# Six projection groups of a hybrid attention and expert block: eight half-matrix products per group become seven, with weight sums formed by accumulating transfers

## The chip, the cores and the metric

One core of a Trainium2 chip runs the whole program. The metric is the device time of one execution in microseconds. The kernel before takes 1276.09 us (median of 3 runs, 1275.9 to 1276.17).

## The reference, cut to what matters

x is 256 x 1024 in float32. It is normalised to h, and one matrix product projects h to 11 parts. Two token mixers use them (a gated delta rule in chunks, and a differential softmax attention over 8 heads), their outputs are gated and added, and an output projection and 32 experts of a clamped SwiGLU follow, of which each token uses 4.

```python
h = rms_norm(x, g_mix[l])
proj = h @ w_in[l]
(qa, ka, va, za, beta_in, a_in, qd, kd, vd, gate_a, gate_b) = jnp.split(proj, split_points, axis=-1)
...
oa = gated_delta_rule(qa, ka, va, beta, g)
oa = rms_norm(oa, g_delta_out[l]) * jax.nn.silu(za.reshape(bsz, seq, H_DELTA, DV_DELTA).astype(jnp.float32))
...
od = diff_attention(qd, kd, vd, lam, rel_bias)
...
mix = jax.nn.sigmoid(gate_a + b_gate[l, 0]) * oa + jax.nn.sigmoid(gate_b + b_gate[l, 1]) * od
x = x + mix @ w_o[l]
```

The six groups that the change touches are qd, kd, vd, za, gate_a and gate_b: each is h (256 x 1024) times a 1024 x 1024 block of w_in.

## The kernel before, in words

Five instruction streams run side by side and meet at semaphores. A list `sched`, written out by hand, gives the order of the work; TensorE, VectorE and ScalarE all walk through it in its order and each engine executes its own part of every item. SyncE has its own order, written beside it.

The front has three stages. First 24 "tile" items project the three delta-rule groups (K, Q, V; L1420). Then 48 "pj" items project the other six groups: group g (QD, KD, VD, Z, GA, GB), row block b of 128 tokens and column half n give a product of 8 steps (128 x 128 by 128 x 512, each two instructions on TensorE, L1430). A pj item is 4 of these 8 steps, thus 8 instructions. The results go to PSUM banks 0 and 1 by turns. ScalarE copies them out (L806, L809); for the gates VectorE does (L1169). The waits for a bank are one whole product apart.

The dictionary `after` hangs other work behind each pj item: the chain of the delta rule (`kt`, `vt`, `n2`, `y1`, `y2`, `y3`, `yt`, `s1`, `ks`, `o0`, `qs`, `o1`; each 8 heads of 16 instructions on L1395, followed by a take of PSUM by VectorE or ScalarE), the inverse of the triangular blocks on VectorE (`sb`, eight pieces behind items 3 to 10, L1084 and L1085), the transposes of q and k (`qt`, `ktd`, L1528), their norms (`nq`, `nk`, L1115 and L1121), and per attention head the steps `a1` (logits), `aw`, `a2` and `a3`. When `sb` is done, SyncE stores the inverse to HBM (L496) and loads it back as diagonal blocks (L502); `n2` of item 11 needs them. `odn` and `oan` scale the mixers' outputs (L1146, L1153), `gate_product` (L1002 to L1005) applies the gates, and `mt` turns the mixed result for the output projection w_o (L1574). Then come the residual, the router and the plan of the experts, up to 371 us.

The third stage walks over 32 experts, w_up first (L1719), then w_down (L1766). Their weights arrive in 192 slabs of 2 MB each, through a ring of 11 slots of 16 KB per partition and a twelfth place beside it. Slabs 0 to 10 are loaded in the front, as soon as what lies in their slot is dead (`front_dead`): slots 8, 9 and 6 hold the projection weights (`w_place`, three pieces of 2 MB in turn), slots 8 and 9 hold w_o until its last product (`s_wo` 3 and 4), slot 10 holds h until the router has run. From 375 us on every load waits for the slab before it in the same slot. All of this is issued by SyncE, in order.

GpSimd squares kd and the delta rule's output in the front (L643, L647), scales that output (L652), issues the load of the gate bias (L649), and is idle in most of the rest.

## Time and profile before

| | |
|---|---|
| time, median of 3 runs | 1276.09 us (1275.9 to 1276.17) |
| span of the profiled execution | 1273.7 us |
| TensorE matmul busy | 1229.8 us, 97% of the span |
| VectorE, ScalarE, GpSimd busy | 373.2, 284.8, 45.9 us |
| moved by DMA | 451.94 MB, mean 355 GB/s |
| granted TensorE clock | 0.999 of full speed |

The profiled execution has no time of its own in the list of runs beside its span; the median of the runs lies 2.4 us above that span. Read it so: TensorE is busy nearly all the time, and the DMA queues are at their full rate (428 to 430 GB/s) in all slices after the first 380 us, but not before. Both engines of the chain are near their limit, in different stretches.

### The profile page before, as it was taken

What the parts mean: (1) busy time and instruction counts of PE and PEld (TensorE: products, weight loads), DVE (VectorE), ACT (ScalarE), POOL (GpSimd) and SP (SyncE); (2) the same over time, 40 slices, a digit from 0 to 9 for tenths busy, and PEclk for the clock granted to TensorE, in tenths of its full rate; (3) what the DMA queues carried; (4) which work ended last, traced back from release to release, by engine and by line L of the source; (5) the groups of instructions that cost most, each with busy time, mean ns of one, the idle gap of its engine ahead of it and who ended that gap; (6) DMA issues with size and microseconds to landing.
All of it is one profiled execution on the core that took longest, in us unless ns stands there. A gap on an engine that the chain in (4) does not pass through costs nothing.

```text
span 1273.7 us, 14917 instructions
## 1 busy us (share of the span) xinstructions
PE 1229.8 (97%) x5590; PEld 539.1 (42%) x5590; DVE 373.2 (29%) x1063; ACT 284.8 (22%) x573; POOL 45.9 (4%) x100
## 2 busy tenths in 40 slices
PE   9999999999999999999999999999998989999997
PEld 7777466644443333333333333333333333333332
DVE  5766825666231211111221111221111112211111
ACT  3331212352222121121121112121121211121121
POOL 4400000101000000000000000000000000000000
PEclk9999999999999999999999999999999999999999
DMA  7653431567779999999999999999999999999997
GB/s 255 181 164 129 147 134 67 181 248 264 274 284 417 425 429 429 429 428 430 429 428 427 429 428 428 428 429 429 429 428 428 428 428 429 429 429 429 428 427 314
DMA packets 60764, 451.94 MB, mean 355 GB/s; under 512 B 10600, under 2 KB 13800, under 8 KB 36032
## 3 DMA queue, kind: packets, MB, share of 16 engines
q1 hardware_dynamic: 59176, 447.44, 85.2%
q0 software_dynamic: 1120, 3.56, 1.0%
q10 hardware_dynamic: 440, 0.58, 0.1%
q8 instruction: 16, 0.26, 0.1%
q14 instruction: 12, 0.10, 0.0%
HBM read 449.21 MB, written 1.97 MB: 354 GB/s over the span
## 4 chain that ended last, share of the span: by engine, by line
PE 66%; DMA 19%; DVE 5%; ACT 3%; issue 1%; SPq 1%; DVEq 0%; ACTq 0%
PE pb L1719 20%; DMA space<-in_w_up_dram 19%; PE pb L1766 14%; PE pb L1430 11%; PE pb L1660 4%; PE pb L1420 3%; PE pb L1647 3%; PE pb L1574 2%; PE pb L1395 2%; PE pb L1654 1%; PE pb L1679 1%; DVE buf_a L1334 1%; DVE buf_a L1331 1%; DVE buf_a L1328 1%; ACT buf_a L898 1%
## 5 line engine op out<-in xcount | busy, mean ns | idle before, releaser
L1719 PE MATMUL pb<-space,buf_a 128*64 128x512 f32 x2048 | 460.4, 595 | 15.5 <-DMA space<-in_w_up_dram 15.4
L1719 PEld LDWEIGHTS pb<-space,buf_a 128*64 128x64 f32 x2048 | 146.1, 137 | 284.8 <-issue 257.3
L1766 PE MATMUL pb<-space 128*64 128x512 f32 x1024 | 227.1, 595 | 7.3 <-ACT space L905 7.3
L1328 DVE TENSOR_SCALAR buf_a<-pb 128x256 f32<-128x256 f32 x64 | 27.0, 421 | 686.7 <-PE pb L1719 686.7
L1430 PE MATMUL pb<-space 128*128 128x512 f32 x384 | 171.4, 594 | 0.0
L1766 PEld LDWEIGHTS pb<-space 128*64 128x64 f32 x1024 | 70.7, 137 | 140.9 <-issue 125.3
L1430 PEld LDWEIGHTS pb<-space 128*128 128x128 f32 x384 | 70.3, 190 | 76.1 <-issue 75.1
L881 ACT ACT_TABLE_LOAD x32 | 41.1, 1283 | 222.5 <-PE pb L1647 222.5
L1420 PE MATMUL pb<-space 128*128 128x256 f32 x384 | 88.6, 384 | 0.9 <-ACT space L734 0.5
L1420 PEld LDWEIGHTS pb<-space 128*128 128x128 f32 x384 | 71.3, 190 | 13.1 <-issue 2.4
L898 ACT ACTIVATE buf_a<-buf_a 128x256 f32<-128x256 f32 x64 | 26.7, 417 | 216.7 <-DVE buf_a L1328 216.7
L1660 PE MATMUL pb<-space 64*128 64x512 f32 x264 | 65.6, 615 | 0.8 <-ACT space L907 0.8
L907 ACT COPY space<-pb 128x512 f32<-128x512 f32 x32 | 18.7, 585 | 209.8 <-PE pb L1766 209.8
L1647 PE MATMUL pb<-xt,plan 128*64 128x512 f32 x248 | 58.7, 592 | 0.0
L898 ACT ACT_TABLE_LOAD x32 | 41.1, 1283 | 0.6
L905 ACT COPY space<-pb 128x256 f32<-128x256 f32 x64 | 24.4, 382 | 70.1 <-PE pb L1679 70.1
L982 DVE SCALAR_TENSOR_TENSOR space<-space 128x255 f32<-128x255 f32 (+2 forms) x72 | 36.3, 504 | 2.6
L1647 PEld LDWEIGHTS pb<-xt,plan 128*64 128x64 f32 x248 | 18.9, 137 | 34.3 <-issue 34.3
L1660 PEld LDWEIGHTS pb<-space 64*128 64x128 f32 x264 | 22.8, 186 | 23.1 <-issue 23.1
L1395 PEld LDWEIGHTS pb<-space 128*128 128x128 f32 x240 | 29.0, 192 | 6.2 <-issue 6.2
L1331 DVE TENSOR_TENSOR buf_a<-buf_a 128x256 f32<-128x256 f32 x64 | 27.2, 425 | 9.7 <-ACT buf_a L898 6.7
L1334 DVE SCALAR_TENSOR_TENSOR buf_a<-buf_a 128x256 f32<-128x256 f32 x64 | 27.3, 426 | 7.9
(299 smaller groups left out, 807.3 us busy)
## 6 DMA issues: line engine op xcount, KB each, us to landing
space<-in_w_up_dram SPq DMA_DIRECT2D x127, 2048.0 KB, 25.7
space<-in_w_down_dram SPq DMA_DIRECT2D x61, 2048.0 KB, 24.2
space<-in_w_in_dram SPq DMA_DIRECT2D x17, 2048.0 KB, 8.0
space<-in_w_o_dram SPq DMA_DIRECT2D x2, 2048.0 KB, 11.9
space<-in_w_down_dram SPq DMA_DIRECT2D x4, 1024.0 KB, 27.3
space<-in_w_down_dram SPq DMA_DIRECT2D x4, 512.0 KB, 16.0
space<-in_w_up_dram SPq DMA_DIRECT2D x2, 1024.0 KB, 41.1
xt<-in_x_dram SPq DMA_DIRECT2D x2, 512.0 KB, 5.3
```

The costliest lines, as they stand in the source:

```text
L881: sc.copy(xgt, pb[:, 3, :]).then_inc(s_xgt, 1)
L898: sc.activation(sgm[:, 256 * n_:256 * n_ + 256], glu[:, 256 * n_:256 * n_ + 256], ACT.Sigmoid, scale=ALPHA).then_inc(s_sgm, 1)
L1328: v.tensor_scalar(glu[:, cols], pairs[:, :, 0], LIMIT, None, ALU.min).then_inc(s_glu, 1)
L1331: v.tensor_tensor(sgm[:, cols], sgm[:, cols], glu[:, cols], ALU.mult).then_inc(s_mdve, 1)
L1334: v.scalar_tensor_tensor(out=act[:, cols], in0=lin[:, cols], scalar=1.0, in1=sgm[:, cols], op0=ALU.add, op1=ALU.mult).then_inc(s_actv, 1)
L1395: ins = mm(psA[:, h], lhs(h), rhs(h), start=True, stop=True)
L1420: ins = mm(pb[:, t % 2, 0:T], w[:, c, (t % 4) * P:(t % 4) * P + P], rows[:, c, :], start=(c == 0), stop=(c == KC - 1))
L1430: ins = mm(pb[:, q % 2, :], hT[:, c, b * P:(b + 1) * P], piece_at(n)[:, c, :], start=(c == 0), stop=(c == KC - 1))
L1647: ins = mm(pb[64 * n_:64 * n_ + 64, 3, :], sel[:, b, :], xt[:, b, 512 * n_:512 * n_ + 512], start=(b == 0), stop=(b == NB - 1), skip_group ...
L1660: return mm(pb[:, 4 + 2 * b + n_, :], GT[rows, b * P:(b + 1) * P], ys[rows, :], start=False, stop=True, skip_group_check=True)
L1719: ins = mm(up_out(hf, n_), xg[:, c, :], up_columns(line, hf, n_), start=False, stop=(c == KC - 1), skip_group_check=True)
L1766: ins = mm(pb[64 * hf:64 * hf + 64, 2, :], actT[:, c // 4 * 2 + c % 2, hf_in, :], slot(m)[:, at_:at_ + 512], start=(c == 0), stop=(c == KC ...
```

## The change: what it does

The six groups are computed by a scheme of seven products of half matrices in place of eight (Winograd's form of Strassen's scheme, one level). h is cut into A11, A12, A21, A22 (row block by half of the 1024 inputs), the weight block into B11, B12, B21, B22. Four sums of the A quarters (SA1 to SA4) are formed once, by GpSimd, and lie in the place of x, which is therefore loaded a second time before the residual. The sums of the B quarters are formed per group in the ring: T starts as a plain load of B11 and then takes three accumulating transfers (`grow` 1 to 3), each after the product that reads the state before it; T3 starts as a load and takes one. The accumulating transfers are issued by GpSimd. Per group there are 5 plain and 4 accumulating transfers of 1 MB, in place of 2 plain ones of 2 MB.

48 pj items become 42 "u" items of the same size (4 steps, 8 instructions of L1430's form): P5, P1, P3, P6, P2, P7, P4 in each group. The two PSUM banks alternate with every unit, and some units accumulate on top of what a unit before left there, so each unit waits for a copy or a result of one or two units before. Per group ScalarE copies four partial results (`COPIED`; for the gates VectorE does, with the bias), and VectorE makes the four outputs from them (`group_result`), one each in P6, P2, P7 and P4.

Squares and the scale of the delta rule's output move from GpSimd to ScalarE and VectorE. The attention's steps stand two items earlier, `qt`, `nq`, `nk` and `ktd` one or two; `odn` is cut in two; `mt` stands behind the last two units. Slab 0 and the next are loaded between the quarters; slot 5 waits for the four gate products of Z. Some semaphores are merged.

```diff
+    UNITS = ("P5", "P1", "P3", "P6", "P2", "P7", "P4")
+    U = {name: j for j, name in enumerate(UNITS)}
+    NU = len(UNITS)
+    NG = 6
+    def quarter_place(g, q):
+        if q == "T":
+            return ((8, 0), (6, 1))[g % 2]
+        return {"B11": (8, 1), "B22": (9, 0), "B21": (9, 1), "T3": (6, 0)}[q]
...
-    items_b = []
-    for g in (QD, KD, VD, Z, GA):
-        items_b += [(g, b, n) for n in range(2) for b in range(NB)]
-    items_b += [(GB, b, n) for b in range(NB) for n in range(2)]
-    no_b = {it: i for i, it in enumerate(items_b)}
...
+    put(8, ("qt", 0))
+    put(9, ("qt", 1), ("nq",))
     put(11, ("n2", 0))
     put(12, ("n2", 1))
     put(13, ("y1", 0))
     put(14, ("y2", 0))
...
-    put(15, ("y3", 0))
-    put(16, ("yt", 0), ("nk",))
-    put(17, ("s1",))
-    put(18, ("ks",), ("ktd", 0))
-    put(19, ("y1", 1), ("ktd", 1))
+    put(15, ("y3", 0), ("nk",))
+    put(16, ("yt", 0), ("ktd", 0))
+    put(17, ("s1",), ("ktd", 1))
+    put(18, ("ks",))
+    put(19, ("y1", 1))
...
+    put(28, ("osum",))
+    put(30, ("osc", 0))
+    put(31, ("osc", 1))
     for h in range(H):
-        put(20 + 2 * h, ("a1", h))
-        put(22 + 2 * h, ("aw", h))
-        put(23 + 2 * h, ("a2", h))
-        put(24 + 2 * h, ("a3", h))
+        put(18 + 2 * h, ("a1", h))
+        put(20 + 2 * h, ("aw", h))
+        put(21 + 2 * h, ("a2", h))
+        put(22 + 2 * h, ("a3", h))
+    put(34, ("odn", 0, 6))
+    put(37, ("odn", 6, 8))
+    put(38, ("oan",))
     for i in after:
         after[i].sort(key=lambda it: {"aw": 0, "a2": 0, "a1": 2}.get(it[0], 1))
-    put(46, ("mt", 0), ("mt", 1))
-    put(39, ("odn",))
-    put(41, ("oan",))
+    put(40, ("mt", 0))
+    put(41, ("mt", 1))
...
-        sched.append(("pj", i // 2, i % 2))
+    for i in range(NU * NG):
+        sched.append(("u", i // NU, i % NU))
...
+        A11, A12, A21, A22 = (hT[:, 4 * k:4 * k + 4, P * b:P * b + P] for b in range(NB) for k in range(2))
+        SA1, SA2, SA3, SA4 = (xt[:, b, 512 * i:512 * i + 512].rearrange("p (c t) -> p c t", c=4) for b in range(NB) for i in range(2))
...
+        FACTORS = {"P5": (SA1, "T"), "P1": (A11, "B11"), "P3": (SA4, "B22"), "P6": (SA2, "T"), "P2": (A12, "B21"), "P7": (SA3, "T3"), "P4": (A22, "T")}
+        def bank_of(g, name):
+            return (g + U[name]) % 2
...
+            def load_quarter(g, q):
+                if g == 0:
+                    sp.wait_ge(s_pj, {"B11": 16, "B22": 20, "B21": 21}[q])
+                else:
+                    sp.wait_ge(s_pj, unit(g - 1, {"B11": "P1", "B22": "P3", "B21": "P2"}[q]))
+                sp.dma_start(quarter_at(g, q), w_quarter(g, q)).then_inc(s_q(q), 16)
+            def begin_sum(g):
+                sp.wait_ge(s_pj, (16, 24)[g] if g < 2 else unit(g - 2, "P4"))
+                sp.dma_start(quarter_at(g, "T"), w_quarter(g, "B11")).then_inc(s_tb[g % 2], 16)
+            def begin_third_sum(g):
+                sp.wait_ge(s_pj, unit(g - 1, "P7") if g else 24)
+                sp.dma_start(quarter_at(g, "T3"), w_quarter(g, "B12")).then_inc(s_t3b, 16)
...
+            begin_sum(QD)
+            load_quarter(QD, "B11")
+            load_quarter(QD, "B22")
+            load_quarter(QD, "B21")
+            sp.wait_ge(s_psAf, nA[("kq", 1, 1)] + 1)
+            for b in range(NB):
+                for d in range(4):
+                    q = 32 * b + 8 * d
+                    sp.dma_start(bass.AP(m_dram, q * 1024, [[32, 32], [1024, 8], [1, 32]]), Mt[32 * d:32 * d + 32, b, :, 32 * d:32 * d + 32]).then_inc(s_mst, 16)
+            sp.wait_ge(s_mst, 16 * 8)
+            sp.wait_ge(s_bup, 1)
+            sp.dma_start(ring[0:64, 0, 0:D], m_dram.ap()).then_inc(s_m32, 16)
+            begin_third_sum(QD)
+            begin_sum(KD)
+            for q in ("B11", "B22", "B21"):
+                load_quarter(KD, q)
+            begin_third_sum(KD)
+            begin_sum(VD)
+            for q in ("B11", "B22"):
+                load_quarter(VD, q)
...
+            load_quarter(VD, "B21")
+            begin_third_sum(VD)
+            begin_sum(Z)
+            for g in (Z, GA):
+                for q in ("B11", "B22", "B21"):
+                    load_quarter(g, q)
+                    if g == GA and q == "B22":
+                        front_dead(0)
+                        load(0)
+                begin_third_sum(g)
+                begin_sum(g + 1)
+            load_quarter(GB, "B11")
+            load_quarter(GB, "B22")
+            front_dead(1)
+            load(1)
+            load_quarter(GB, "B21")
+            begin_third_sum(GB)
+            front_dead(2)
+            load(2)
+            sp.wait_ge(s_pj, unit(GB, "P1"))
+            load_w_o(0, 0)
+            load_w_o(0, 1)
+            front_dead(3)
+            load(3)
+            sp.wait_ge(s_pj, unit(GB, "P3"))
+            load_w_o(1, 0)
+            sp.wait_ge(s_pj, unit(GB, "P2"))
+            load_w_o(1, 1)
+            load(4)
+            sp.wait_ge(s_pj, unit(GB, "P7"))
+            for b in range(NB):
+                sp.dma_start(xt[:, b, :], x[0, b * P:(b + 1) * P, :]).then_inc(s_x[b], 16)
...
+            link(pool.tensor_tensor(SA1, A21, A22, ALU.subtract))
+            link(pool.tensor_tensor(SA2, SA1, A11, ALU.subtract))
+            pool.tensor_tensor(SA3, A11, A21, ALU.subtract).then_inc(s_hT, 1)
+            pool.tensor_tensor(SA4, A12, SA2, ALU.add).then_inc(s_hT, 1)
...
+            def grow(g, n):
+                if n == 1:
+                    pool.wait_ge(s_tb[g % 2], 16 * (g // 2 + 1))
+                else:
+                    pool.wait_ge(s_pj, unit(g, ("P5", "P6")[n - 2]))
+                    pool.wait_ge(s_t[g % 2], grown(g, n - 1))
+                pool.dma_start(quarter_at(g, "T"), w_quarter(g, ("B12", "B22", "B21")[n - 1]), accum_op=ALU.add).then_inc(s_t[g % 2], 16)
+            def grow_third(g):
+                pool.wait_ge(s_t3b, 16 * (g + 1))
+                pool.dma_start(quarter_at(g, "T3"), w_quarter(g, "B22"), accum_op=ALU.add).then_inc(s_t3, 16)
+            grow(QD, 1)
+            grow(QD, 2)
+            grow_third(QD)
+            grow(KD, 1)
...
+            grow(QD, 3)
+            for g in range(KD, NG):
+                grow(g, 2)
+                grow_third(g)
+                if g == Z:
+                    pool.wait_ge(s_psA, nA[("y3", 1)] + 1)
+                    pool.dma_start(gbias, b_gate.to_broadcast([P, 2, D])).then_inc(s_ml, 16)
+                if g < GB:
+                    grow(g + 1, 1)
+                grow(g, 3)
...
+            COPIED = {"P5": 2, "P1": 1, "P3": 0, "P7": 3}
+            USED = {"P2": 0, "P7": 1, "P4": 2}
+            LAST_USED = {"P6": 0, "P2": 1, "P7": 2, "P4": 3}
...
+                    if name in COPIED and g < GA:
+                        k = COPIED[name]
+                        act_e.wait_ge(s_pj, unit(g, name))
+                        if name == "P5" and g == VD:
+                            act_e.wait_ge(s_psA, nA[("vt", 1)] + 1)
+                        elif name == "P5" and g == Z:
+                            act_e.wait_ge(s_red, 2)
+                        sc.copy(group_out(g, k), pb[:, bank_of(g, name), :]).then_inc(s_pjf, 1)
+                    if g == GB and name in LAST_USED:
+                        use(g, LAST_USED[name])
+                    elif g < GB and name in USED:
+                        use(g, USED[name])
+                    if name == "P5" and g:
+                        use(g - 1, 3)
...
+            def group_result(g, name):
+                k = RESULT[name]
+                dst, src = group_out(g, k), pb[:, bank_of(g, name), :]
+                dve.wait_ge(s_pj, unit(g, name))
+                if name == "P6":
+                    dve.wait_ge(s_pjf, copied(g, 3))
+                    ins = v.tensor_tensor(dst, dst, src, ALU.subtract)
+                elif name == "P2":
+                    dve.wait_ge(s_pjf, copied(g, 2))
+                    ins = v.tensor_tensor(dst, src, dst, ALU.add)
+                elif name == "P7":
+                    if g < GA:
+                        dve.wait_ge(s_pjf, copied(g, 4))
+                        src = group_out(g, 3)
+                    ins = v.tensor_tensor(dst, dst, src, ALU.subtract)
+                else:
+                    dve.wait_ge(s_pjf, copied(g, 4))
+                    ins = v.tensor_tensor(dst, src, dst, ALU.add)
+                ins.then_inc(s_cf, 1)
...
+                    g, name = it[1], UNITS[it[2]]
+                    if g > Z and name == "P5":
+                        gate_product(g - 1, 2)
+                    if name in RESULT:
+                        group_result(g, name)
+                    if g >= GA and name in COPIED:
+                        if g == GA and name == "P5":
+                            dve.wait_ge(s_ml, 64)
+                        take_with_bias(g, name, COPIED[name])
+                    if g > Z and name == "P1":
+                        gate_product(g - 1, 3)
+                    elif g >= Z and name == "P7":
+                        gate_product(g, 0)
+                    elif g >= Z and name == "P4":
+                        gate_product(g, 1)
+                        if g == GB:
+                            gate_product(g, 2)
+                            gate_product(g, 3)
...
+                    rows, q = FACTORS[name]
+                    bank = bank_of(g, name)
+                    if name == "P5":
+                        if g == 0:
+                            pe.wait_ge(s_pjf, 23)
+                            pe.wait_ge(s_hT, 4)
+                        else:
+                            pe.wait_ge(s_pjf, copied(g - 1, 4))
+                        pe.wait_ge(s_t[g % 2], grown(g, 1))
+                    elif name == "P1":
+                        if g == 0:
+                            pe.wait_ge(s_pjf, 24)
+                        else:
+                            pe.wait_ge(s_cf, 4 * g)
+                        pe.wait_ge(s_q(q), loaded(g, q))
+                    elif name == "P3":
+                        pe.wait_ge(s_pjf, copied(g, 1))
+                        pe.wait_ge(s_q(q), loaded(g, q))
+                    elif name == "P6":
+                        pe.wait_ge(s_pjf, copied(g, 2))
+                        pe.wait_ge(s_t[g % 2], grown(g, 2))
+                    elif name == "P2":
+                        pe.wait_ge(s_pjf, copied(g, 3))
+                        pe.wait_ge(s_q(q), loaded(g, q))
+                    elif name == "P7":
+                        pe.wait_ge(s_cf, 4 * g + 1)
+                        pe.wait_ge(s_t3, 16 * (g + 1))
+                    else:
+                        pe.wait_ge(s_cf, 4 * g + 2)
+                        pe.wait_ge(s_t[g % 2], grown(g, 3))
+                    cols = quarter(g, q).rearrange("p (k n) -> p k n", k=4)
+                    opens = name in ("P5", "P1", "P2", "P4")
+                    for c in range(4):
+                        ins = mm(pb[:, bank, :], rows[:, c, :], cols[:, c, :], start=(opens and c == 0), stop=(c == 3), skip_group_check=True)
+                    ins.then_inc(s_pj, 1)
```

## Rows read from the trace of the kernel before

**Rows 1.** The page: the span, and GB/s in 40 slices of 31.8 us.
```profile
span 1273.7 us, 14917 instructions
...
GB/s 255 181 164 129 147 134 67 181 248 264 274 284 417 425 429 429 429 428 430 429 428 427 429 428 428 428 429 429 429 428 428 428 428 429 429 429 429 428 427 314
```

**Rows 2.** The chain that ended last: start us, us, what; an early pair and late ones.
```profile
426.55 6.87 PE pb L1719 x32
...
481.36 6.87 PE pb L1719 x32
...
921.85 39.52 DMA space<-in_w_up_dram
...
1212.10 38.15 DMA space<-in_w_up_dram
```

**Rows 3.** Windows: stretch, length, busy of PE, PEld, DVE, ACT, POOL, PEclk, DMA share, GB/s.
```profile
260.00:280.00 20.00, 19.29 (x70) 9.79 (x69) 11.83 (x38) 12.79 (x45) 0.00 (x0) 1.00 0.70 276
...
340.00:350.00 10.00, 9.76 (x29) 4.65 (x28) 2.03 (x8) 3.88 (x8) 1.85 (x4) 1.00 0.99 420
350.00:360.00 10.00, 10.00 (x42) 5.85 (x41) 3.15 (x11) 1.79 (x4) 0.00 (x0) 1.00 0.70 250
360.00:370.00 10.00, 9.21 (x54) 5.48 (x52) 6.53 (x29) 3.83 (x10) 0.00 (x0) 1.00 0.70 264
...
380.00:390.00 10.00, 9.62 (x46) 3.50 (x44) 3.10 (x9) 3.98 (x5) 0.00 (x0) 1.00 1.01 433
```

**Rows 4.** Timeline of PE in the front: start us, us, engine line op xcount.
```profile
126.59 24.20 PE L1430 MATMUL pb<-space 128*128 128x512 f32 x56
...
159.25 1.95 PE L1395 MATMUL pb<-space 128*128 128x128 f32 x16
161.03 3.60 PE L1430 MATMUL pb<-space 128*128 128x512 f32 x8
...
329.90 7.03 PE L1574 MATMUL pb<-space 128*128 128x512 f32 x16
...
371.56 7.04 PE L1719 MATMUL pb<-space,buf_a 128*64 128x512 f32 x32
```

**Rows 5.** Timeline of DVE, the inverse (first and last of 31 pairs) and the norm behind it.
```profile
129.07 0.18 DVE L1084 TENSOR_TENSOR space<-space 64x31 f32<-64x31 f32 x1
...
151.71 0.18 DVE L1085 TENSOR_TENSOR space<-space 64x31 f32<-64x31 f32 x1
151.82 2.27 DVE L1115 TENSOR_REDUCE sm<-space 128x32 f32<-128x2048 f32 x1
...
158.60 0.19 DVE L929 TENSOR_TENSOR sm<-sm 128x32 f32<-128x32 f32 x1 [3.90 <-ACT sm L686]
```

**Rows 6.** Timeline of SP's queue: the inverse is stored and loaded back.
```profile
151.93 0.49 SPq L496 DMA_DIRECT2D t_blocks<-space  x1
154.82 3.78 SPq L502 DMA_DIRECT2D space<-t_blocks  x8
```

**Rows 7.** Timeline of DVE, later steps.
```profile
193.49 2.36 DVE L1127 TENSOR_TENSOR space<-space,sm 128x1024 f32<-128x1024 f32 x2
...
277.58 0.69 DVE L1169 TENSOR_TENSOR space<-pb,space 128x512 f32<-128x512 f32 x1
...
306.00 4.29 DVE L1146 SCALAR_TENSOR_TENSOR buf_a<-buf_a,sm,space 128x128 f32<-128x128 f32 x16
...
322.97 0.68 DVE L1004 SCALAR_TENSOR_TENSOR buf_a<-space,buf_a 128x512 f32<-128x512 f32 x1
323.69 0.69 DVE L1005 TENSOR_TENSOR buf_a<-buf_a,space 128x512 f32<-128x512 f32 x1
```

**Rows 8.** DMA of the page and its view: issues, KB each, us from issue to landing.
```profile
q0 software_dynamic: 1120, 3.56, 1.0%
...
space<-in_w_in_dram SPq DMA_DIRECT2D x17, 2048.0 KB, 8.0
...
space<-in_b_gate_dram POOLq DMA_DIRECT2D x1, 1024.0 KB, 6.9
```

313 lines of the change are left out of this document (152 added, 161 removed).

## The prediction

> **What bounds the kernel now.** I read the page first. From the thirteenth slice on the DMA queues move 417 to 430 GB/s in every slice but the last [rows 1]; that is their limit. The chain of waits says the same: from 922 us on its longest pieces are waits for w_up slabs, such as 39.5 and 38.2 us [rows 2]. Until then TensorE runs one expert in 27.4 us (426.55 to 481.36 for a pair [rows 2]), while 12.58 MB of slabs per expert take 29.3 us at 429 GB/s, so the ring, filled in the front, slowly drains. The end is therefore set by when the queues become full for good, plus what is left to move. The windows show that moment: 420 GB/s at 340 to 350 us, then 250 and 264 while slots 8, 9 and 10 are still in use, and 433 from 380 [rows 3]. Those slots, and the refills behind them, are released by TensorE's progress (the last products of w_o, the router, the first expert). So TensorE's front, from 113.7 us (first pj item) to 371.56 us (first expert, [rows 4]), sets the start of the full stream, and a microsecond won or lost there moves the end by one, as long as the queues have nothing left over from the front. In this front TensorE waits for nearly nothing: seven items in a row in 24.2 us, and w_o starts at 329.90, right behind the last item [rows 4].
>
> **Fewer products.** An item of eight instructions takes 3.44 us: 24.04 us for seven [rows 4]. 48 items become 42: 6 x 3.44 = 20.6 us off the path. All work behind the items stays, partly two items earlier, so it takes the same TensorE time. This is the whole gain; everything else can only cost.
>
> **The inverse comes late.** VectorE's 31 pairs of L1084 and L1085 run from 129.07 to 151.89, 22.8 us without a pause [rows 5]. Then SyncE stores (151.93), loads back from 154.82 (four loads of half a row block issued by 156.7), and `n2` starts at 159.25 [rows 4, 6]: some 7 us behind the end of the pairs, with practically no slack. In the new order `n2` still stands behind item 11, and the items before it are equally many and long, with the two `qt` before it as before; TensorE would be there at 159.25 again. But VectorE now has to make results between the pieces of the inverse. The first piece stands behind the result of P6 (item 3), which ends at 126.59 + 3.44 = 130.0, and a result costs 0.69 us like L1169 [rows 7]; so it starts at 130.8. Between the pieces stand three more results of QD (2.1 us, and 1.4 us of waiting for P2's end and for ScalarE's copy of P7), then, ahead of the last piece, `nq` and the result of KD's P6. `nq` took 2.27 us for the reduction and until 159.46 in all, of which 3.90 us waited for ScalarE [rows 5]; ScalarE should now be less late, so I take 4.1 us, and 0.7 for the result. 130.8 + 22.8 + 3.5 + 4.1 + 0.7 = 161.9 against 151.9. With the same way through HBM (6.6 us) `n2` can start at 168.5, 9.2 us late. No other work is queued on TensorE ahead of it. Bounds: 6 us (if `nq` costs only its 2.3 us and the copies are early) to 13 us (`nq` as long as before).
>
> **`nk` before `yt`.** `nk` moves in front of `yt`'s take; `ktd` needs its first half. From the end of `y3` it takes 1.22 (the take) + 2.8 (reduction and two small steps) + 0.6 (ScalarE's root) + 0.9 (four small steps) + 1.2 us (half of the 2.36 us of L1127 [rows 7]) = 6.7 us; TensorE has 3.44 + 1.78 us of work (item, then 159.25 to 161.03 for `yt` [rows 4]). Cost 1.5, bounds 0 to 3.
>
> **The end of the projections.** Before, the gates' last products were covered by a pj item. Now VectorE has, behind item 34, a result (0.7), a gate product (0.7), `aw` (four passes, some 1.8) and twelve of the sixteen operations of `odn` (4.29 x 12/16 = 3.2 us [rows 7]) with its root (1.4), some 7.8 us, and only then the two copies with bias that item 37 waits for: 9.2 us against 7.9 us of TensorE work, cost 1.3. Behind item 40 stand a result, a copy with bias and a gate product of two operations, 0.69 + 0.69 + 1.4 = 2.8 us, before `mt` 0 can run; behind item 41 a result, a gate product, then `mt` 1 and ScalarE's copy, 0.7 + 1.4 + 0.5 + 0.6 = 3.2 us, before w_o can start [rows 7]. Nothing is queued on TensorE to cover these. Together 7.3, bounds 4 to 9. The bank handovers elsewhere have one unit (3.44 us) of cover for a 0.6 or 0.7 us copy; between the heads of the attention VectorE is busy for 11.83 of 20 us, ScalarE for 12.79 [rows 3], and VectorE gets some 1 us per two units more. I take 0; up to 4 if its long items fall badly.
>
> **The transfers.** The before has no accumulating transfer. The nearest row is the gate bias, 1 MB from GpSimd's queue, 6.9 us from issue to landing; 2 MB of w_in land in 8.0 [rows 8]. Lower bound for one: 6.9 us, like a plain one. If the destination has to be read too, it costs the time of 1 MB more at 429 GB/s, 2.4 us: 9.3; upper bound two plain ones in turn, 13.8. I take 9.3, as an addition needs both operands. The windows that the schedule leaves: `grow` 2 two units with what lies behind them (9.4 us in QD), `grow` 3 two units (6.9 us in QD and GB, more between). In QD `grow` 3, issued at 130.2, stands in GpSimd's queue behind T3 and KD's first sum, 4.9 us of data each, issued at about 125 and 127. It lands near 142, 5 us late for item 6, and item 6's result moves the inverse by 3.8. As a plain transfer it would be 0.4 late. In GA and GB the windows of 8 to 10 us meet slabs 0 to 4 and w_o on the other queue (2 MB, 4.9 us each): I take 3 us together, bounds 0 to 12. Sum 6.8, bounds 0.5 to 18. The bytes: 5 more MB-blocks in six groups and x are 32.5 MB or 76 us of full queue, 135 us with second reads. The slices from 64 to 318 us leave room for 156 us [rows 1], so the stream is not delayed at the lower price and hardly at the higher.
>
> The Trainium skill, "Collectives: The Full Stack", the bandwidth ceiling (fold count), says that a reducing transfer is slow because it makes two reads for one write, not because of the addition, with a measured ratio of 1.93. By that rule a chain of such transfers would run at about half the rate, which is the 9.3 us, not the 6.9 us; no row here can show it. The sum with 6.9 us would be 1276.
>
> **The clock.** All windows of the front show a granted clock of 1.00 [rows 3], but none has a wait of 9 us. After this one the next unit and step (3.44 + 1.78) might run at the lower level, 1.2 GHz: 0 to 5.2 us, I take 2. The Trainium skill, "TensorE: Matmul & The Clock Gate", Part 1, states that the clock falls to half when TensorE idles and comes back after work; the rows only show it never idle for long.
>
> **The sum.** -20.6 + 9.2 + 1.5 + 7.3 + 0 + 6.8 + 2 = +6.2 us. The second load of x (1 MB, issued 3.4 us before the last unit ends, needed after the first w_o product, 7 us long, and the 3.2 us before it) and GpSimd's four sums (about 1 us each, at some 60 us, long before item 0) cost nothing; if slabs ahead of x delayed it by more than 4 us, the residual would wait. ScalarE's squares replace GpSimd's, off the path. The profiled span would go from 1273.7 to 1279.9 us; the median lay 2.4 us above the span, 1276.09 + 6.2 = 1282.3.
>
> **Rivals.**
> 1. The handovers on VectorE fit better than I lay them out (the inverse 6 late, the end 4, the rest 0) and accumulating costs as a plain transfer: -20.6 + 6 + 0 + 4 + 0.5 = -10, 1266; with half of these, 1270. For it: ScalarE and VectorE are idle most of the time, and before 240 us the queues are half empty. Against it: the 22.8 us of the inverse are unbroken, and its order behind item 3 is fixed. Chance 0.32, by all cases that end below 1273.5.
> 2. The costs cancel the gain, 1276: the sum with accumulation as cheap as plain, and a steady clock. Chance 0.15.
> 3. The queues decide: an accumulating transfer takes 13.8 us and over, so that in every group `grow` 2 and 3 miss windows of 7 to 9 us by 3 us or more once the other queue is busy. 18 us of transfers in place of 6.8 gives 1294; it decides from a landing time of about 10 us on. Chance 0.15.
> 4. My forecast, 1282.3 (own range 1279 to 1289): 0.38.
> A last one, that the change doesn't do what it says, has no chance worth a number: the items are counted in the schedule.
>
> **How the numbers follow.** Likeliest is case 4. Range: down to 1267 (most of rival 1), up to 1298 (rival 3 with some of the bounds above). A measurement of this kernel tells 0.2%, 2.6 us, from no change: faster 0.32, same 0.15, slower 0.53.
>
> **What would show it.** Right: 336 instructions of the projection in the place of 384; TensorE idle for 6 to 13 us ahead of `n2` with the inverse's end near 162 and the load-back as its releaser; gaps of about 3 us before each `mt` or w_o; the first expert 4 to 9 us later than 371.56. Landing times from GpSimd's queue of 9 us or more support the transfers' term, 7 us refute it. Wrong: an `n2` that starts at 160, or a first expert before 368 us; or a first expert early but an end that isn't, which would mean that the queues carried a backlog over the front.

## The result and the profile after

The changed kernel takes 1348.46 us (median of 4 runs, 1347.71 to 1351.16), the kernel before 1276.13 us on the same chip: ratio 1.0567, 95% interval 1.0552 to 1.0582, 72.3 us slower. The forecast was 1282.3 us with a range up to 1298. The sign was right, the size was wrong by 66 us. In the profiled execution the span grew from 1273.7 to 1346.0 us, also by 72.3.

The page of the kernel after: the span, the clock and the DMA line in 40 slices of 33.7 us, the two large queues, the chain of waits, and the issues (KB each, us from issue to landing).

```profile
span 1346.0 us, 14958 instructions
...
PEclk9999788999789999999999999999999999999999
DMA  8554997898897999999999999999999999999997
GB/s 264 187 137 118 264 211 171 228 279 229 270 340 286 381 428 428 428 428 428 428 428 428 427 428 428 428 428 429 428 428 428 428 428 428 429 428 428 428 428 324
...
q1 hardware_dynamic: 62856, 454.78, 82.0%
q0 software_dynamic: 13792, 28.73, 11.4%
...
PE pb L1955 19%; DMA space<-in_w_up_dram 18%; PE pb L2002 14%; DMA space<-in_w_in_dram 9%; PE pb L1667 6%; PE pb L1896 4%; PE pb L1630 3%; PE pb L1883 3%; PE pb L1810 2%; PE pb L1605 1%; PE pb L1890 1%; PE pb L1915 1%; DVE buf_a L1541 1%; DVE buf_a L1544 1%; DVE buf_a L1538 1%
...
space<-in_w_in_dram SPq DMA_DIRECT2D x31, 1024.0 KB, 12.5
space<-in_w_in_dram POOLq DMA_DIRECT2D x24, 1024.0 KB, 16.4
```

From the fifteenth slice on, the queues are as full as before from the thirteenth [rows 1]. In slices 5 to 12 they are 70 to over 90% busy, yet move only 171 to 340 GB/s: busy, but at a low rate. The chain now holds 9% of waits for w_in, which before it did not name. The 24 accumulating transfers (growths, below) land 16.4 us after their issue (the median); 9.3 us was my price. The page also counts the 336 projection instructions that the change promised, 144 and 192 on L1667, in the place of 384.

The timeline of TensorE from the first item of the new stage to the first expert (start us, us, engine, line, operation, tiles; in brackets the idle time before it and what ended it). It answers [rows 4].

```profile
120.01 3.60 PE L1667 MATMUL pb<-space,xt 128*128 128x512 f32 x8
...
135.74 3.67 PE L1667 MATMUL pb<-space,xt 128*128 128x512 f32 x8 [2.64 <-DMA space<-in_w_in_dram]
...
150.29 6.29 PE L1667 MATMUL pb<-space,xt 128*128 128x512 f32 x8 [7.45 <-DMA space<-in_w_in_dram]
...
165.03 5.75 PE L1667 MATMUL pb<-space 128*128 128x512 f32 x8 [8.45 <-DMA space<-in_w_in_dram]
...
206.03 3.75 PE L1605 MATMUL pb<-space 128*128 128x128 f32 x16 [15.00 <-issue]
...
305.40 5.54 PE L1667 MATMUL pb<-space 128*128 128x512 f32 x8 [6.89 <-DMA space<-in_w_in_dram]
...
352.67 5.79 PE L1667 MATMUL pb<-space 128*128 128x512 f32 x8 [13.70 <-DMA space<-in_w_in_dram]
...
393.55 5.83 PE L1667 MATMUL pb<-space 128*128 128x512 f32 x8 [6.38 <-DMA space<-in_w_in_dram]
...
444.65 7.04 PE L1955 MATMUL pb<-space,buf_a 128*64 128x512 f32 x32
```

The first item starts at 120.0 instead of 113.7, the first expert at 444.65 instead of 371.56 [rows 4]: 73.1 us, and the end moved by 72.3. The whole loss lies in the front. Within the stage TensorE waits some 72 us: 48.5 us for quarters of w_in (the P4 unit of four groups, P7 of the first one, and some small ones) and 15.0 us ahead of `n2` (the row at 206.03). Behind each of the five waits of 6.4 to 13.7 us for w_in eight instructions take 5.5 to 6.3 us instead of 3.6, and behind `n2` sixteen small ones take 3.75 instead of 1.95: that is the lower of the two clock levels (1.2 instead of 2.4 GHz), some 13 us behind six waits. It does not grow with the wait: 2.7 us behind 7.45, 2.2 behind 13.70, and almost nothing (0.07) behind 2.64.

The windows of the same stretches (columns as in [rows 3]) show the granted clock at 0.77 and 0.83 where it had been 1.00:

```profile
150.00:200.00 50.00, 31.19 (x72) 13.90 (x72) 22.39 (x57) 8.20 (x12) 5.17 (x4) 0.77 0.90 213
...
350.00:400.00 50.00, 35.29 (x83) 15.51 (x83) 21.64 (x52) 10.81 (x22) 3.87 (x3) 0.83 0.95 295
```

The DMA view of the whole front (105 to 420 us: bytes and share of the 16 engines' time):

```profile
q1 hardware_dynamic: 22388, 51.67, 45.0%
q0 software_dynamic: 12288, 25.17, 43.3%
...
t_blocks<-space SPq DMA_DIRECT2D x1, 256.0 KB, 9.9
```

GpSimd's queue moved half the bytes of the other and took as much of the engines: 0.433 x 315 = 136 us for 25.17 MB (24 transfers of 1 MB, of which 23 add and one is the gate bias). The 256 KB store of the inverse, which landed within 2.9 us before (SyncE issued the loads back right behind it [rows 6]), took 9.9.

### The profile page after: what moved, and what is told of

Same layout as the page of the kernel before. It is cut to its first block, busy times and chain, and to the rows that moved or that the text cites. A ratio compares the mean times of both kernels' runs of the same rounds, so it can differ in the third digit from the quotient of the medians.

```text
span 1346.0 us, 14958 instructions
## 1 busy us (share of the span) xinstructions
PE 1228.1 (91%) x5542; PEld 537.8 (40%) x5542; DVE 391.3 (29%) x1081; ACT 296.9 (22%) x598; POOL 70.3 (5%) x121
## 3 DMA queue, kind: packets, MB, share of 16 engines
HBM read 481.71 MB, written 1.97 MB: 359 GB/s over the span
## 4 chain that ended last, share of the span: by engine, by line
PE 57%; DMA 28%; DVE 4%; issue 3%; ACT 2%; SPq 1%; POOL 0%; DVEq 0%; ACTq 0%; POOLq 0%
PE pb L1955 19%; DMA space<-in_w_up_dram 18%; PE pb L2002 14%; DMA space<-in_w_in_dram 9%; PE pb L1667 6%; PE pb L1896 4%; PE pb L1630 3%; PE pb L1883 3%; PE pb L1810 2%; PE pb L1605 1%; PE pb L1890 1%; PE pb L1915 1%; DVE buf_a L1541 1%; DVE buf_a L1544 1%; DVE buf_a L1538 1%
## 5 line engine op out<-in xcount | busy, mean ns | idle before, releaser
L1955 PE MATMUL pb<-space,buf_a 128*64 128x512 f32 x2048 | 460.4, 595 | 14.8 <-DMA space<-in_w_up_dram 14.7
L1667 PE MATMUL pb<-space 128*128 128x512 f32 x144 | 73.6, 658 | 35.8 <-DMA space<-in_w_in_dram 35.8
L1667 PE MATMUL pb<-space,xt 128*128 128x512 f32 x192 | 90.2, 614 | 13.5 <-DMA space<-in_w_in_dram 12.8
L1630 PE MATMUL pb<-space 128*128 128x256 f32 x384 | 91.3, 392 | 4.4 <-ACT space L907 4.0
L1630 PEld LDWEIGHTS pb<-space 128*128 128x128 f32 x384 | 73.3, 195 | 17.4 <-ACT space L907 4.3
L1667 PEld LDWEIGHTS pb<-space 128*128 128x128 f32 x144 | 29.4, 213 | 70.4 <-issue 70.2
L1667 PEld LDWEIGHTS pb<-space,xt 128*128 128x128 f32 x192 | 35.9, 197 | 53.9 <-issue 52.3
L1605 PE MATMUL pb<-space 128*128 128x128 f32 x240 | 31.0, 285 | 15.0 <-issue 15.0
L778 POOL DMA_DIRECT2D space<-in_w_in_dram x18 | 26.7, 1485 | 264.2 <-PE pb L1667 240.9
L1152 DVE SCALAR_TENSOR_TENSOR space<-space 128x255 f32<-128x255 f32 (+2 forms) x72 | 39.3, 546 | 2.6
L1605 PEld LDWEIGHTS pb<-space 128*128 128x128 f32 x240 | 30.5, 201 | 21.1 <-issue 21.1
## 6 DMA issues: line engine op xcount, KB each, us to landing
space<-in_w_in_dram POOLq DMA_DIRECT2D x24, 1024.0 KB, 16.4
```

Source lines behind the costliest of these rows:

```text
L1152: ins = v.scalar_tensor_tensor(out=a[:, d:], in0=src[:, 0:T - d], scalar=conv_c[:, 3 - d, tap:tap + 1], in1=a[:, d:], op0=ALU.mult, op1=AL ...
L1605: ins = mm(psA[:, h], lhs(h), rhs(h), start=True, stop=True)
L1630: ins = mm(pb[:, t % 2, 0:T], w[:, c, (t % 4) * P:(t % 4) * P + P], rows[:, c, :], start=(c == 0), stop=(c == KC - 1))
L1667: ins = mm(pb[:, bank, :], rows[:, c, :], cols[:, c, :], start=(opens and c == 0), stop=(c == 3), skip_group_check=True)
L1955: ins = mm(up_out(hf, n_), xg[:, c, :], up_columns(line, hf, n_), start=False, stop=(c == KC - 1), skip_group_check=True)
```

## The experiments

Each row gives the difference of the time from the kernel before on the same chip, the difference of the profiled spans, and the start of the first expert against 371.56. Span and first expert agree within 1.0 us, time and first expert within 1.9: the end follows the front.

| kernel | time | minus before | span minus 1273.7 | first expert minus 371.56 |
|---|---|---|---|---|
| after | 1348.46 | +72.3 | +72.3 | +73.1 |
| f2: inverse one item earlier | 1351.96 | +76.2 | +77.6 | +76.6 |
| f1: four sums later | 1343.06 | +67.3 | +68.7 | +68.4 |
| f3: third growth first | 1337.80 | +62.1 | +63.2 | +63.2 |
| g4: f1, f2 and f3 together | 1329.07 | +52.9 | +53.4 | +53.6 |
| f4: sums on GpSimd | 1321.13 | +45.4 | +46.3 | +45.8 |
| g3: 2 of 4 sums on VectorE, groups 2 to 6 | 1309.60 | +33.4 | +33.4 | +33.2 |
| e2: transfers without addition | 1302.2 (one run) | +25.8 | +26.8 | +26.6 |
| g5: g3 in all groups | 1291.93 | +15.5 | +16.1 | +16.0 |
| g1: no accumulating transfers | 1288.27 | +12.1 | +13.4 | +13.1 |
| g2: g1, and the orders of f1 and f2 | 1271.87 | -4.3 | -1.9 | -2.4 |

### The price of the transfer by itself (e1)

The kernel only moves 1 MB quarters of w_in: plain from SyncE, plain and accumulating from GpSimd, one by one, three in a row, and beside six loads of SyncE's queue.

> A small kernel that computes nothing of the block: it only moves quarters of w_in (1 MB, rows of 2 KB), one after the other. Theory: an accumulating transfer takes more than twice a plain one's data time even alone; in the changed kernel the GpSimd queue was busy for 43.3% of 315 us with 24 of them, 5.7 us of all 16 engines for each, against 2.4 us for 1 MB at 429 GB/s. So 6 to 7 us plain, 10 us or more accumulating, and three issued together take 6 us more for each. Rival (they are only late because of what is queued beside them): 7 us alone, 2.5 us more for each further one.

GpSimd's timeline, where each issue but those of L61 waits for the landing of the one before (L55 plain, L58 accumulating, L61 three accumulating at once, L63 accumulating beside six loads, L66 plain beside six loads, L70 accumulating with 8 KB rows):

```profile
48.10 0.77 POOL L55 DMA_DIRECT2D space<-in_w_in_dram  x1 [5.08 <-DMA space<-in_w_in_dram]
54.02 0.75 POOL L55 DMA_DIRECT2D space<-in_w_in_dram  x1 [5.15 <-DMA space<-in_w_in_dram]
59.69 1.31 POOL L58 DMA_DIRECT2D space<-in_w_in_dram  x1 [4.92 <-DMA space<-in_w_in_dram]
68.62 1.28 POOL L58 DMA_DIRECT2D space<-in_w_in_dram  x1 [7.62 <-DMA space<-in_w_in_dram]
77.24 1.27 POOL L58 DMA_DIRECT2D space<-in_w_in_dram  x1 [7.34 <-DMA space<-in_w_in_dram]
86.17 3.87 POOL L61 DMA_DIRECT2D space<-in_w_in_dram  x3 [7.67 <-DMA space<-in_w_in_dram]
105.22 1.29 POOL L63 DMA_DIRECT2D space<-in_w_in_dram  x1 [15.19 <-DMA space<-in_w_in_dram]
```

Alone, an accumulating transfer lands in 8.6 us, a plain one of the same queue in 5.6, one of SyncE's in 5.1. Three issued 0.75 us apart land 8.5, 12.8 and 17.2 us after their issue, so one landing follows the other by some 5.1 us. Beside six loads, one takes 14.6 (a plain one 9.7). So neither theory had it: alone it is cheaper than the theory's 10 us and dearer than the rival's 7, and each further one lies between their 6 and 2.5 us. The price alone was even under my 9.3; what I had not priced was company. In the changed kernel, company is the rule.

### Where the addition's share lies (e2, g1)

In e2 the 24 transfers overwrite their place instead of adding to it, so the sums of quarters are not formed; bytes read, issues and waits stay.

```diff
-  pool.dma_start(quarter_at(g, "T"), w_quarter(g, ("B12", "B22", "B21")[n - 1]), accum_op=ALU.add).then_inc(s_t[g % 2], 16)
+  pool.dma_start(quarter_at(g, "T"), w_quarter(g, ("B12", "B22", "B21")[n - 1])).then_inc(s_t[g % 2], 16)
```

> The changed kernel with the addition left out of the 24 accumulating transfers: same bytes, same queue, same waits; the last quarter then overwrites the sum, so six projections are wrong. Theory (the second read and the addition are the price): landing times fall from 16.4 to about 8 us, the waits of TensorE for w_in from 48.5 to under 10 us, and the time to 1285 to 1295 us. Rival (the bytes and the software queue are the price, not the addition): stays at 1335 to 1350 us.

It took 1302.2 us (one run), 7 us beyond the theory's range and far from the rival's: 46 us of the 72 go with the addition alone. The transfers landed after 7.8 us and the waits for w_in fell to 8.8 us, both as the theory had them. The engines' share, in the DMA view of its front (105 to 390 us), shows how:

```profile
q1 hardware_dynamic: 22597, 54.17, 52.0%
q0 software_dynamic: 6464, 25.30, 24.3%
```

The same 25 MB take 0.243 x 285 = 69 us of the 16 engines instead of 136, so each MB costs 1.97 times the engines' time when it is added. It is not the crowd that makes it so: in e1, where nothing else runs, three plain transfers take 53.5% of the engines from 42.0 to 59.6 us (9.4 us) and three accumulating ones 71.8% from 59.7 to 86.1 us (19.0 us), twice as much. The Trainium skill, "Collectives: The Full Stack", the bandwidth ceiling (fold count), has a measured 1.93 between the copying and the reducing step of a ring of cores and explains it by two reads for one write; the traces here agree with the ratio for a transfer from HBM to SBUF, and no run here looks at the reads.

In e3 the 24 transfers are left out (the semaphores are raised without them), so the sums are only their first quarters.

```diff
-  pool.dma_start(quarter_at(g, "T"), w_quarter(g, ("B12", "B22", "B21")[n - 1]), accum_op=ALU.add).then_inc(s_t[g % 2], 16)
+  pool.sem_inc(s_t[g % 2], 16)
```

> The changed kernel without its 24 accumulating transfers, their counts raised at once by GpSimd: T stays B11, T3 stays B12, so six projections are wrong. Theory: what is left is the gain of 20.6 us, the early loss of 6.3 us (GpSimd's four sums block VectorE) and VectorE's order (inverse 9.2, ktd 1.5, end 7.3, clock 2): 1282 us, between 1278 and 1286. Rival (VectorE's order costs little, everything was the transfers): 1262 us.

The other values sent more than 64 tokens to one expert, so the kernel went over the experts twice (2227 us), and only its front can be read: first expert at 380.49, 8.9 us late, which fits the theory's 1278 to 1286. g1 is the same kernel with the number of rounds held at one:

> The kernel without the 24 additions (only the first quarter of each sum is loaded, so the outputs of the projections are not the reference's) with the number of rounds over the experts held at one, as in the kernel before, so that its total can be compared. Its first expert started 8.9 us later than before in the trace. Theory (the end follows the front one to one): 1282 to 1288 us. Rival (24 MB of reads less leave the stream a lead that the front doesn't show): under 1280 us.

1288.27 us, ratio 1.0091 (1.0075 to 1.0108): 0.3 us above what the theory gave. Its first expert started at 384.64, 4 us later than in e3 with the same instructions and, within 0.1 us, the same waits. Three rows of g1 show where it went:

```profile
288.17 5.06 PE L1667 MATMUL pb<-space,xt 128*128 128x512 f32 x8
...
332.83 4.83 PE L1667 MATMUL pb<-space 128*128 128x512 f32 x8
...
341.20 8.80 PE L1810 MATMUL pb<-space 128*128 128x512 f32 x16 [0.77 <-ACT space L868]
```

In e3 the same three take 3.70, 3.60 and 7.10 us. With the short rows beside them, g1 lost 1.7 us at each of the three places, 5.1 in all, less the 0.8 us by which it was ahead at 286 us: the granted clock of 280 to 300, 320 to 340 and 340 to 360 us is 0.91 in g1 and 1.00 in e3. So behind the same waits of 2.4 us, of 2.7, and of 2.1 and 0.8 close together, the clock fell in one execution and not in the other. A front with waits in it is thus known only to some 4 us from one profile. In sum: of 72 us, 46 are the addition, 14 (1302.2 to 1288.3) the 24 MB, their issues and their waits as plain transfers, and 12 are there without any of them. Of the 14, e2's timeline shows 8.8 us as three waits for w_in (3.09, 4.54 and 1.14), and most of the rest as more time at the lower clock.

### The queue of three (f3, g4)

After P5 of a group GpSimd issued its second growth, its third sum, and the first growth of the next group; the third growth of this group, needed two items after P6, stood behind them. In f3 the next group's growth comes last.

```diff
                 grow(g, 2)
                 grow_third(g)
-                if g < GB:
-                    grow(g + 1, 1)
                 grow(g, 3)
+                if g < GB:
+                    grow(g + 1, 1)
```

(and for the first group likewise)

> The changed kernel with one edit: the first growth of the next group's sum is queued behind the third growth of the present one instead of ahead of it, so that two accumulating transfers instead of three stand together. Theory (a queue of accumulating transfers, each about 4.4 us more when issued together, and more beside loads): the waits ahead of P4 (8.5, 6.9, 13.7 and 6.4 us in the trace) shrink by 4 to 8 us each, the sum of waits by 15 to 30 us, and the time to 1318 to 1335 us. Rival (it is the traffic of all queues together, not the order): the waits only move from P4 to the next P5, and the time stays within 8 us of 1348.

1337.80 us, ratio 1.0482 (1.0465 to 1.05): 10.7 us less, under what the theory gave (13 to 30) and over the rival's 8. The timeline shows why both are half right:

```profile
157.70 2.81 PE L1667 MATMUL pb<-space 128*128 128x512 f32 x6 [2.36 <-DMA space<-in_w_in_dram]
...
164.52 5.07 PE L1667 MATMUL pb<-space,xt 128*128 128x512 f32 x8 [3.15 <-DMA space<-in_w_in_dram]
...
337.03 3.75 PE L1667 MATMUL pb<-space 128*128 128x512 f32 x4 [8.26 <-DMA space<-in_w_in_dram]
345.11 3.67 PE L1667 MATMUL pb<-space,xt 128*128 128x512 f32 x8 [1.55 <-DMA space<-in_w_in_dram]
```

(The first and the third row are cut at the edge of their window.) The P4 waits fell from 8.45 to 2.36 and from 13.70 to 8.26, and new waits of 3.15 and 1.55 us came at the next P5: part of each wait only moved. All waits for w_in fell from 48.5 to 37.6 us. The order was one cause; the addition itself (46 us in e2) is the larger one.

### GpSimd's four sums (f1)

The four sums of turned quarters, which I had put down as free, move from tile 6 to one behind each of tiles 12 to 15.

```diff
-            link(pool.tensor_tensor(SA1, A21, A22, ALU.subtract))
+            pool.wait_ge(s_pj, 12)
+            link(pool.tensor_tensor(SA1, A21, A22, ALU.subtract))
```

> The changed kernel with one edit: GpSimd's four sums of turned quarters (each 1.27 to 1.44 us, at 55.85 to 61.28 us in its trace) move from the sixth tile to tiles 12 to 15, one behind each tile. Theory (the lock): they cost 6.3 us because they stood where VectorE's chain sets the pace (three of its additions took 4.25 us instead of 1.58); one per tile is absorbed by the pauses of 1 to 2 us that VectorE has per tile, so the first item of the new stage starts 6 us earlier, at 114 us, and the time falls by 5 to 7 us to 1342 to 1344 us. Rival A (the waits on transfers give the time back, since the transfers don't start earlier): the stage starts earlier but the time falls by less than 2 us. Rival B: the lock costs as much at any place: no change.

In the kernel after, VectorE's timeline has this row beside them; the same operations take 1.52 to 1.58 us elsewhere:

```profile
57.31 4.25 DVE L1152 SCALAR_TENSOR_TENSOR space<-space 128x255 f32<-128x255 f32 x3
```

TensorE's timeline shows what came of it:

```profile
67.95 6.52 PE L1630 MATMUL pb<-space 128*128 128x256 f32 x16 [3.97 <-ACT space L907]
```

ScalarE waited for VectorE, and TensorE for ScalarE: 3.97 us, 0.48 before, and the sixteen instructions behind it took 6.52 us at the lower clock, 3.72 before. So 3.5 of the 6.3 us are VectorE's delay, and 2.8 are the clock.

With the move the first item started at 113.59 instead of 120.01, and the time fell by 5.4 us to 1343.06 (ratio 1.0531, 1.0513 to 1.0549), as the theory had it. Where VectorE has pauses, the same four operations cost nothing (113.59 against 113.67 us before).

### The inverse one item earlier (e4, f2)

```diff
-        put(3 + i, ("sb", 4 * i, min(4 * i + 4, 31)))
+        put(2 + i, ("sb", 4 * i, min(4 * i + 4, 31)))
-    put(9, ("qt", 1), ("nq",))
+    put(9, ("qt", 1))
+    put(10, ("nq",))
```

First on top of e3, without accumulating transfers (two rounds again, so only the front counts), then alone in the changed kernel:

> As e3_no_growth, with the eight pieces of the inverse one item earlier (behind items 2 to 9) and nq behind item 10. Theory: n2 waits 3 us in place of 10, the time falls by 6 to 10 us against e3_no_growth. Rival (the inverse is not what n2 waits for, or TensorE's wait there is absorbed elsewhere): no change, within 1 us.

> The changed kernel, accumulating transfers and all, with one edit: the pieces of the triangular inverse stand one item earlier in VectorE's order and the reduction of the first group behind item 10. In the kernel without the 24 additions this moved the first expert 9.3 us forward. Theory: the wait of 15.0 us at n2 falls by 7 to 9 us and the time with it, to 1339 to 1342 us. Rival: the inverse's end is not what is late beside the slow store (9.9 us), or the transfers' waits right behind grow by what n2 gives: under 3 us.

In e4 the wait at `n2` fell from 8.35 to 1.22 us and the first expert came at 371.19, 9.3 us earlier. In f2 it gave nothing: 1351.96 us, 3.5 us more than the kernel after (the runs of the two overlap), with 15.98 us of waiting at `n2`. My theory fell, and SyncE's timeline of f2, with the DMA view of 180 to 204 us, and then the same two rows of the kernel after say why:

```profile
182.78 0.64 SPq L595 DMA_DIRECT2D t_blocks<-space  x1
201.72 3.81 SPq L601 DMA_DIRECT2D space<-t_blocks  x8
```

```profile
q0 software_dynamic: 1792, 3.57, 80.6%
q1 hardware_dynamic: 1136, 2.36, 29.4%
...
t_blocks<-space SPq DMA_DIRECT2D x1, 256.0 KB, 18.9
```

```profile
190.69 0.49 SPq L594 DMA_DIRECT2D t_blocks<-space  x1
200.63 3.89 SPq L600 DMA_DIRECT2D space<-t_blocks  x8
```

The inverse was stored 7.9 us earlier, but it landed no earlier: at 201.7 us, 200.6 in the kernel after. In both, GpSimd's growths hold 80% of the engines around the store. The last of the three issued together from 174.6 us on (174.9 in f2), and the quarter of w_in that stands ahead of the store in SyncE's queue, land only at about 199.5 us (200.5 in f2), and the store some 1 us behind them. It waited for the end of this burst, and an earlier issue only lengthened the wait, from 9.9 to 18.9 us. How much of it is the shared engines and how much the quarter ahead in the same queue, no run separates. In g4, with f3's order, the store still took 15 us:

> The whole computation with all sums by accumulating transfers, and the three edits of order together: the third growth queued ahead of the next group's first, the four sums of turned quarters behind tiles 12 to 15, the inverse's pieces one item earlier. Alone they gave -10.7, -5.4 and +3.5 us. Theory (the inverse's edit gave nothing because its store waited 18.9 us behind accumulating transfers; with fewer of them in the queue at that time it gives 0 to 8 us): 1323 to 1333 us. Rival (the gains overlap in the same waits): 1334 to 1340 us.

1329.07 us (ratio 1.0414, 1.0397 to 1.0432), in the theory's range: the three edits together gave 19.4 us, more than the 12.6 that they add up to alone. But `n2` still waited 14.8 us, so the theory's reason, that the inverse's edit begins to pay, is not what the trace shows.

### Adding on the chip (f4, g3, g5)

If the transfer is the trouble, the quarters that lie in SBUF can be added there. f4 loads each quarter once and lets GpSimd add (the first group keeps its transfers; the orders of f1 and f2 are in, as in g3 and g5, and here the order of f3 too):

```diff
+  for k in range(4):
+      ins = pool.tensor_tensor(t_[:, k], t_[:, k], b_[:, k], ALU.add)
```

> The sums of the last five groups formed on the chip: each of the four quarters is loaded once (4 MB a group instead of 7), and GpSimd adds them from SBUF (T = B12 + B11, then + B22, T3 = T - B11, then T + B21), four pieces of 128x512 each; the first group keeps its accumulating transfers; with the two edits of order (the four sums behind tiles 12 to 15, the inverse's pieces one item earlier). Theory (the accumulating transfers and their bytes are the loss): an addition of 2048 elements takes GpSimd 5.2 us, 21 us in a group of 36 us and always two items ahead of its reader; the first expert starts at 362 to 372 us and the time is 1266 to 1277 us. Rival (the lock between GpSimd and VectorE): VectorE's operations with two inputs in SBUF stretch beside 104 us of additions, and PE waits for VectorE instead: 1282 to 1300 us.

1321.13 us (ratio 1.0337, 1.0306 to 1.0368): better than any version with transfers alone, but beyond the rival's range. The waits for w_in were gone behind the first group. VectorE's timeline shows the end of the inverse while GpSimd adds; a row of 64x31 takes 0.18 us when it doesn't [rows 5]:

```profile
177.98 1.19 DVE L1323 TENSOR_TENSOR space<-space 64x60 f32<-64x60 f32 x1
179.20 1.15 DVE L1322 TENSOR_TENSOR space<-space 64x31 f32<-64x31 f32 x1
180.39 0.18 DVE L1323 TENSOR_TENSOR space<-space 64x31 f32<-64x31 f32 x1
```

Each of VectorE's two-input operations takes about as long as one of GpSimd's 128x512 pieces, however small it is. They alternate: from 170.4 to 180.3 us GpSimd made eight pieces (1.24 us each; 1.36 in the four from 158.3 on) and VectorE eight operations. The inverse ended at 180.6, `n2` waited 13.1 us, and later steps of VectorE made TensorE wait 8.4, 5.5 and 4.3 us. The Trainium skill, "SBUF — State Buffer", SBUF: two separate sides, calls this an exclusive lock on a shared port pair, held for a whole instruction, between a VectorE operation with two SBUF inputs and a GpSimd operation that reads SBUF; the rows agree.

In g3 VectorE itself makes the second and third addition to T in the last five groups; the rest stays with transfers.

```diff
+  v.tensor_tensor(quarter(g, "T"), quarter(g, "T"), quarter(g, q), ALU.add).then_inc(s_add, 1)
```

> The whole computation, with both edits of order; in the five groups behind the first the second and third addition to T (B22, B21) are made by VectorE from the quarters that lie in SBUF, one operation of 2048 elements each, while the first addition and the third sum stay accumulating transfers, which have six items of time; 7 MB a group instead of 9. Theory (what hurts is the accumulating transfer on a path of three items, and GpSimd's lock on VectorE where it adds itself): an addition takes VectorE 2.1 to 2.4 us, no wait of PE for a transfer over 3 us is left behind the first group, n2 waits 3 to 6 us; the first expert starts at 370 to 382 us and the time is 1274 to 1288 us. Rival (VectorE becomes the bound in the attention stage, where it was busy 11.8 of 20 us): waits for VectorE of 10 us and more in sum, 1290 to 1305 us.

1309.60 us (ratio 1.0266, 1.0249 to 1.0283), above the theory's 1274 to 1288 and above the rival's 1290 to 1305 too. The rival's mechanism is a part of it: TensorE waited 16.3 us for VectorE, with `n2`, against 8.1 in g2 with the same orders. An addition took 2.29 us as expected, and behind the first group no wait for a transfer was left; but the first group, left as it was, cost 2.8, 7.4 and 8.3 us of waiting and some 5 us of the lower clock behind them, the larger part. g5 takes its two additions off the transfers as well, and issues the load that begins its third sum ahead of the wait for the stores of the inverse's blocks. (The 400.8 us that its expectation names for g3 is the step just ahead of the first expert, which itself started at 404.75; held against the first expert, its range of 378 to 386 us was missed by 1.5 us.)

> As the kernel with VectorE's additions, whole computation, but in the first group too VectorE makes the second and third addition, and the load that begins that group's third sum stands ahead of the wait for the stores of the inverse's blocks. Theory (the first group's accumulating transfers are most of what is left): PE's waits of 2.8, 7.4 and 8.3 us there fall to under 4 us in sum, the half clock behind them goes (5 to 8 us), n2 waits 4 us longer (two additions of 2.3 us in the inverse's path): the first expert starts at 378 to 386 us, 400.8 without this edit, and the time is 1286 to 1296 us, still slower than before because VectorE's 12 additions (27 us) stand in its path and PE waits for it at n2. Rival (VectorE's additions cost as much as the transfers did): 1300 us or more. Rival (nothing but the transfers was wrong): as the kernel with free sums, 1276 us or less.

1291.93 us (ratio 1.0125, 1.0108 to 1.0142), the step at 383.58 and the first expert at 387.51 us; the time is in the theory's range. Its timeline of TensorE shows the only wait for w_in that is left, and the longest wait of all:

```profile
136.91 3.67 PE L1683 MATMUL pb<-space,xt 128*128 128x512 f32 x8 [2.25 <-DMA space<-in_w_in_dram]
...
172.64 3.75 PE L1621 MATMUL pb<-space 128*128 128x128 f32 x16 [7.48 <-issue]
```

The one ahead of `n2` has again a store of 10.1 us in it, beside 42% of the engines on GpSimd's queue. VectorE's 12 additions are 27.4 us, and TensorE waits for VectorE in other places: 4.08 and 2.11 us at the two `mt`, 2.27 and 1.61 at units whose sum it makes.

### What the scheme could give at most (g2)

> The same without the additions and held at one round, with both edits of order (the four sums of turned quarters behind tiles 12 to 15, the inverse's pieces one item earlier): what the change could give at most in this form, if its sums were free. Theory: the first expert starts at 364 to 368 us, 371.56 before, and the time is 1267 to 1273 us. Rival (the six products saved go where something else is late, as VectorE at n2 and ahead of w_o): no faster than before, 1274 us or more.

1271.87 us, ratio 0.9957 (0.994 to 0.9973), within the theory's range, though its first expert at 369.14 is later than the 364 to 368 it named: 4.3 us faster than before, with sums that cost nothing at all. Its runs spread from 1268.86 us, with a granted clock of 1.00, to 1273.5 with 0.996; the profiled one is the slowest. These 4.3 us are the prize for which the transfers were paid. No version with the whole computation beat the kernel before; the nearest, g5, is 1.25% slower.

## Why the prediction was wrong, point by point

- **The end follows the front.** Right, and shown eleven times over in the table.
- **Fewer products, -20.6 us.** Right: in g2 the waits that are left (1.04 at `n2`, 1.40, 1.33, 2.44, 0.79, 2.71, 2.11 and 0.77) are 12.6 us, and the lower clock took 1.8 more in w_o (8.80 against 7.03 [rows 4]) and 1.5 behind `mt` 0 (1.12 and 4.63 us for rows that take 0.65 and 3.60 in e3); -20.6 + 12.6 + 1.8 + 1.5 = -4.7, and the front came 2.4 us earlier. The 2.3 us between them were not traced.
- **`ktd`, `mt` and w_o.** Right: 1.40 us (1.5 forecast), 2.70 ahead of `mt` 0 (2.8), 2.11 and 0.77 behind it (3.2), 0.78 at item 37 (1.3).
- **The handovers between heads, 0.** Small miss, inside my "up to 4": ScalarE lets TensorE wait 1.33 and 2.44 us in g1.
- **The inverse, 9.2 us.** Right without the transfers, in size and in reason: `n2` waits 8.35 us in e3 and 8.30 in g1, and e3 stores the inverse at 167.9, where 161.9 and the 6.3 us of late start give 168.2. In the kernel after it is 15.0, because I took the way through HBM from [rows 6], where the queues were half empty. The store's 2.9 us became 9.9, and I had let no transfer of the new ones touch it.
- **GpSimd's four sums, 0.** Wrong: 5.4 us (f1), up to 6.4 at the first item. I asked only when their result was needed, not which engine they hold up while they run. The row to ask was VectorE's timeline from 56.1 to 63.0 us before, which has no idle time over 0.2 us and and behind which ScalarE and TensorE come late in the kernel after.
- **The transfers, 6.8 us, bounds 0.5 to 18.** This is the step that failed. I had put their cost at 6.8 us; together with the waits and the clock behind them it is 60 us (1348.46 less g1's 1288.27). Three errors in one term. First, the price: 9.3 us for one was near (8.6), but it is a price alone; beside loads it is 14.6, and in the kernel 16.4. I had taken the condition "over 10 us" as a rival with 0.15 and priced it at 18 us, though with 17 to 22 us of landing (330.02 to 352.5 for the third growth of GA) the P4 of four groups miss their windows by 6 to 14. Second, the queue: I followed three growths in line in the first group only, with 4.9 us each (5.1 measured), and not in the others, where the same order stands in the loop. Third, the bytes: I compared 135 us with a room of 156 us and concluded that nothing is delayed. The room is a sum over 254 us, and 42 of the 156 us lie ahead of 127 us, where only the first two of the 24 additions are issued (88.3 and 123.9 us). Behind it, up to the 318 us to which I counted, the room was 114 us, less than the 135. And the demand comes in bursts right behind P5 and P6, and the windows between 150 and 400 us are 84 to 95% busy. Engines that are 90% busy have room on average and none when it is needed.
- **The clock, 2 us.** Mis-sized: some 13 us. It was sized for one wait; there were six in the stage, and a seventh at 68 us with 2.8 us behind it (f1). It came once for each wait of 3.97 to 15.0 us, at 1.9 to 2.8 us whatever the length, so it grew with the number of waits; the shorter waits of g1 and e3 had it in one execution and not in the other.
- **The Trainium skill's ratio of 1.93** (the place named above). I used it to choose between 6.9 and 9.3 us for one landing. As a ratio of the engines' time for an added MB it was right (1.97). My "135 us" for all new bytes together was right in size too: the two queues took 51.2% of the front before (105 to 371 us, 136 us) and 88.3% of the front after (105 to 420 us, 278 us), 142 us more. I had the sum and set it aside.
- **The rivals.** Rival 3 had the mechanism and the deciding point right, though the growths missed their windows in four groups and not in every one. Its price covered growths that miss their windows alone, without the queue of three, the slow store and the clock.

What stays open: why behind the same short waits the clock fell in g1 and not in e3, how much of e2's waits is the issue on GpSimd and how much the engines, and whether the inverse's store is held up by the engines or by the quarter ahead of it in its queue. Whether fewer w_up loads during the front would have helped the growths wasn't tried.
